# Opening of an encoder kernel: weight row 0, norm gains and token tile 0 as one buffer, loaded by halves of the partitions

## The reference

```
h = concatenate([meta, x], axis=1)            # 272 tokens x 1024
a = rmsnorm(h, g[0])                          # y = x * rsqrt(mean(x*x) + eps) * g
proj = a @ w_in                               # q, k, v, g of 4 heads
q = rotary(q, pos); k = rotary(k, pos)        # cos and sin of position x frequency
```

## Time and profile before

| | |
|---|---|
| median of 3 runs | 696.47 us (696.41 to 696.52) |
| profiled execution, its own time | 696.7 us |
| its span, first to last instruction | 694.9 us |
| TensorE busy | 688.1 us (99%) |
| VectorE busy | 618.9 us (89%) |
| ScalarE busy | 522.3 us (75%) |
| HBM read | 129.23 MB |

### The profile page before, as it was taken

One profiled execution on the slowest core, in us unless ns is written; L12 is line 12 of the kernel. 1 busy time (PEld: TensorE's weight loads), 2 busy tenths in 40 slices (PEclk: granted clock), 3 DMA queues, 4 the chain that ended last, 5 costly groups with the idle time before them and its releaser, 6 DMA issues.

```text
span 694.9 us, 15951 instructions
## 1 busy us (share of the span) xinstructions
PE 688.1 (99%) x6471; PEld 579.0 (83%) x6471; DVE 618.9 (89%) x868; ACT 522.3 (75%) x851; POOL 25.2 (4%) x26
## 2 busy tenths in 40 slices
PE   9999999999999999999999999999999999999997
PEld 7888888888999888888889998888888888884454
DVE  6989898978989799998998889999999999999533
ACT  7477867767755888987888677999878888897441
POOL 0002010100110000000003000000000000000000
PEclk9999999999999999999999999999999999999999
DMA  9875656462643455655589941110545656566821
GB/s 345 325 256 155 246 147 252 139 216 105 220 206 121 154 213 191 232 203 199 202 331 384 354 148 62 62 61 1 182 166 199 237 195 224 199 232 220 256 41 61
DMA packets 48635, 134.51 MB, mean 194 GB/s; under 512 B 30784, under 2 KB 31296, under 8 KB 33344
## 3 DMA queue, kind: packets, MB, share of 16 engines
q1 hardware_dynamic: 48288, 133.39, 54.8%
q10 hardware_dynamic: 288, 0.31, 0.1%
HBM read 129.23 MB, written 1.05 MB: 187 GB/s over the span
## 4 chain that ended last, share of the span: by engine, by line
PE 96%; DVE 2%; DMA 1%; issue 1%; ACT 0%; POOLq 0%; DVEq 0%; SPq 0%; ACTq 0%
PE ps L1894 25%; PE ps L1895 25%; PE ps L1896 25%; PE ps L2397 3%; PE ps L2395 3%; PE ps L2396 3%; PE ps L2329 1%; PE ps L1926 1%; PE ps L1947 1%; PE ps L1927 1%; PE ps L2042 1%; PE ps L2049 1%; PE ps L2044 1%; DMA stage<-in_chunks 1%; PE ps L2145 1%
## 5 line engine op out<-in xcount | busy, mean ns | idle before, releaser
L1894 PE MATMUL ps<-a_hi,w_hi 128*128 128x272 f16 (+1 forms) x1008 | 279.2, 277 | 0.2 <-DVE w_lo L1097 0.2
L1895 PE MATMUL ps<-a_lo,w_hi 128*128 128x272 f16 (+1 forms) x1008 | 279.1, 277 | 0.0
L1896 PE MATMUL ps<-a_hi,w_lo 128*128 128x272 f16 (+1 forms) x1008 | 279.1, 277 | 0.0
L1097 DVE SCALAR_TENSOR_TENSOR w_lo<-stage,w_hi 128x1024 f16<-128x1024 f32 x205 | 247.4, 1234 | 20.6 <-ACT w_hi L566 20.2
L566 ACT ACTIVATE w_hi<-stage 128x1024 f16<-128x1024 f32 x205 | 207.8, 1046 | 49.8 <-PE ps L2397 18.3
L1894 PEld LDWEIGHTS ps<-a_hi,w_hi 128*128 128x128 f16 x1008 | 98.6, 98 | 16.8 <-DVE w_lo L1097 0.5
L1896 PEld LDWEIGHTS ps<-a_hi,w_lo 128*128 128x128 f16 x1008 | 98.6, 98 | 16.1
L1895 PEld LDWEIGHTS ps<-a_lo,w_hi 128*128 128x128 f16 x1008 | 98.6, 98 | 16.0
L1894 PE MATMUL ps<-y_hi,w_hi 128*128 128x272 f16 (+3 forms) x496 | 106.1, 242 | 0.0
L1895 PE MATMUL ps<-y_lo,w_hi 128*128 128x272 f16 (+3 forms) x496 | 106.0, 242 | 0.0
L1896 PE MATMUL ps<-y_hi,w_lo 128*128 128x272 f16 (+3 forms) x496 | 106.0, 242 | 0.0
(11 more groups left out here) (320 smaller groups left out, 1074.9 us busy)
## 6 DMA issues: line engine op xcount, KB each, us to landing
stage<-in_chunks SPq DMA_DIRECT2D x118, 1024.0 KB
work<-work SPq DMA_DIRECT2D x96, 32.0 KB, 2.1
stage<-in_chunks SPq DMA_DIRECT2D x6, 256.0 KB
decay_all<-in_decay SPq DMA_DIRECT2D x1, 1056.0 KB, 11.9
out<-sq SPq DMA_DIRECT2D x4, 256.0 KB, 2.0
hT<-in_tokens SPq DMA_DIRECT2D x3, 272.0 KB, 5.5
stage<-in_chunks SPq DMA_DIRECT2D x1, 512.0 KB
mT<-in_gains SPq DMA_DIRECT2D x1, 512.0 KB, 6.7
```

The costliest lines, as they stand in the source:

```text
L1097: dve.scalar_tensor_tensor(out=part(1, c, q), in0=flat(stage, c, q), scalar=W_SCALE, in1=part(0, c, q), op0=ALU.mult, op1=ALU.subtract).th ...
L1894: pe.matmul(o, w_h, x_h, start=start, stop=False)
L1895: pe.matmul(o, w_h, x_l, start=False, stop=False)
L1896: return pe.matmul(o, w_l, x_h, start=False, stop=stop)
```

## The change

Weight row 0, the norm gains and token tile 0 now stand side by side in one buffer, 512 + 64 + 272 = 848 float32 on each partition, and side by side in the input array too. The upper 64 partitions are loaded by ScalarE's queue, the lower 64 by SP's. ScalarE (for `w_hi` of row 0) and VectorE (for `a_hi` of tile 0) wait until both halves have landed (`x_landed[0]` at 32). SP no longer loads row 0 from the weight array. The place of weight row 0 in the buffer is shared with the rotation table, which is loaded into it later; SP waits for `w_lo` of row 0 (`even_low`) before it issues that load. The total size of the buffers is the same.

```
+OPENING = CW + 8 * DT + T
...
-        hT_all = sb("hT", [P, 8 * DT + DT * T])
-        hT = hT_all[:, 8 * DT:].rearrange("p (a b) -> p a b", b=T)
+        rope_first = sb("rope_first", [P, 2 * T - CW + OPENING + (DT - 1) * T])
+        rope_sb = rope_first[:, 0:2 * T].rearrange("p (a b) -> p a b", b=T)
+        hT_all = rope_first[:, 2 * T - CW:]
+        first_row = hT_all[:, 0:CW]
+        hT = hT_all[:, CW + 8 * DT:].rearrange("p (a b) -> p a b", b=T)
...
-        rope_sb = sb("rope_sb", [P, 2, T])
...
-        gains_sb = hT_all[:, 0:8 * DT]
+        gains_sb = hT_all[:, CW:CW + 8 * DT]
...
-        row_landed = {k: sem(f"row_landed{k}") for k in (0, 1, 2, 4, 5)}
+        row_landed = {k: sem(f"row_landed{k}") for k in (1, 2, 4, 5)}
...
-                at = P * (8 * DT + dt * T)
+                at = P * (OPENING + (dt - 1) * T)
...
             first_chunk = chunks[0:2 * P, :].rearrange("r n -> (r n)")
-            for k0, count in FIRST_ROWS:
+            sp.dma_start(hT_all[0:P // 2, 0:OPENING],
+                         tokens[0:P // 2 * OPENING].rearrange("(p n) -> p n", p=P // 2)).then_inc(x_landed[0], 16)
+            for k0, count in FIRST_ROWS[1:]:
...
                 if c == 1:
-                    sp.dma_start(rope_sb[:], rope).then_inc(table_landed, 16)
+                    sp.wait_ge(even_low, 1)
+                    sp.dma_start(rope_sb, rope).then_inc(table_landed, 16)
                     sp.dma_start(ident_sb[:], ident).then_inc(ident_landed, 16)
...
                     if dt < KC - 2:
-                        if dt in row_landed:
+                        if dt == 0:
+                            act.wait_ge(x_landed[0], 32)
+                        elif dt in row_landed:
                             act.wait_ge(row_landed[dt], 32)
                         else:
                             act.wait_ge(w_landed[0][dt // 4], 32)
-                        act.activation(w_hi[0][:, dt, :], stage[0][:, dt, :], ACTF.Copy,
+                        act.activation(w_hi[0][:, dt, :], stage[0][:, dt, :] if dt else first_row, ACTF.Copy,
                                        scale=W_SCALE).then_inc(whi_made if dt % 2 else even_high, 1)
...
-            for n, (a, b) in enumerate(((0, 8 * DT + T), (8 * DT + T, 8 * DT + 2 * T))):
-                act.dma_start(hT_all[:, a:b], tokens[P * a:P * b].rearrange("(p n) -> p n", p=P)).then_inc(x_landed[n], 16)
+            act.dma_start(hT_all[P // 2:P, 0:OPENING],
+                          tokens[P // 2 * OPENING:P * OPENING].rearrange("(p n) -> p n", p=P // 2)).then_inc(x_landed[0], 16)
+            act.dma_start(hT[:, 1, :], tokens[P * OPENING:P * (OPENING + T)].rearrange("(p n) -> p n",
+                                                                                       p=P)).then_inc(x_landed[1], 16)
...
-            dve.wait_ge(x_landed[0], 16)
+            dve.wait_ge(x_landed[0], 32)
...
-                    dve.scalar_tensor_tensor(out=w_lo[0][:, dt, :], in0=stage[0][:, dt, :], scalar=W_SCALE,
+                    dve.scalar_tensor_tensor(out=w_lo[0][:, dt, :], in0=stage[0][:, dt, :] if dt else first_row, scalar=W_SCALE,
...
-    pieces[0] = np.concatenate([columns(inputs["norm_gains"]), pieces[0]], 1)
+    pieces[0] = np.concatenate([inputs["ret_w_in"][0][0:P, 2 * D:2 * D + CW], columns(inputs["norm_gains"]), pieces[0]], 1)
```

## The result

| kernel | median us | lowest to highest | runs |
|---|---|---|---|
| before | 696.49 | 696.11 to 696.92 | 22 |
| changed | 697.28 | 697.00 to 699.93 | 22 |

What follows compares the result with a forecast made beforehand. TensorE, busy 99% of the span, bounds the kernel; row 0's data hold back its start, at most 0.44 us. Of that 0.33 us was taken to survive row 2, other edits 0: 696.47 - 0.33 = 696.14 us, range 695.8 to 696.9.

Steps and rivals of the forecast that it cites:

- The bound: Start of TensorE's products: at most 0.09 + 0.35 = 0.44 us to win, held back only by row 0's data.
- In the lull the engines lack packets: Opening loads, 2.4 to 2.8 us: half-idle engines at 204 GB/s; 3392 B packets at 120 a us would give 407 GB/s.
- Sharing the opening evenly alone is worth up to 0.36: Opening loads: SP's queue ran ahead of ACT's; an even split would start VectorE near 4.05 us rather than 4.39.
- The opening is through after 434 / 399 = 1.09 us: Opening loads: 434 KB at the full pace of 399 GB/s from about 1.8 us, so VectorE starts at 3.5.
- row 2 decides what passes: Weight row 2: no slack, so only its earlier landing survives as gain; 0.33 us taken, between 0.23 and 0.44.
- The accounting by packets for row 1: Token tile 1: queues share by packets, so 835 KB pass 0.33 us earlier and row 1's w_hi is ready at 5.96.
- Smaller edits at nothing: SP's issue and new wait, buffer placement, w_hi and w_lo work: bounded by -0.1 to +0.1 us, taken as 0.
- That half a transfer's issue might be shorter: SP's queue: if issue goes by partitions, 64 partitions save half an issue, 0 to 0.25 us of SP's time.
- Rival (b): Opening loads: the two halves hinder each other, row 2 starts 0.3 to 0.5 us later, 696.8 to 697.0; chance 0.16.
- they alternate on each engine: Argument against slower halves: both queues would have to be hampered alike throughout, while alternating on each engine.
- The 0.12 us for a product on the lower level: TensorE's first products: one moved onto the 1.2 GHz level would cost 0.12 us; no loss seen, warm-ups stand ahead.
- the case "within": Whole kernel: measured time within 0.2%, 1.4 us, of no change; chance 0.97.

Runs made afterwards that it cites:

- One transfer: Changed kernel, but the whole 848-column opening buffer loaded by one 128-partition transfer on SP's queue: 696.85 us, ratio 1.0005.
- the buffer alone: Changed kernel's shared buffer, layout and SP wait, but the loads of before and ScalarE waiting for the weight row alone: 696.46 us, ratio 0.9999.
- By columns: Changed kernel, but the two queues share the opening buffer as 128 partitions x 424 columns each: 696.70 us, ratio 1.0002.

## Why the prediction was wrong, step by step

- **The bound** (0.44 us to be won at most) was not tested, since no encoder run had its inputs sooner by more than 0.14 us; that row 0 is held by its data stands. It has a reverse side that I didn't use: where nothing is slack, whatever comes late is paid in full.
- **"In the lull the engines lack packets", the opening is through sooner with larger ones: wrong, and here the forecast gain failed.** I read 120 packets a us as a limit in packets. One transfer with the same 3392 B packets moved 148 GB/s from 2.4 to 2.8 us, the changed kernel 178, and the buffer alone 317 with the packets of before. Few packets at half-idle engines were not a sign that wider packets would help, and the lull wasn't even a constant of these loads.
- **"Sharing the opening evenly alone is worth up to 0.36": wrong.** By columns the share is even, and VectorE started at 4.40 against 4.39.
- **The halves taken as equal to whole rows: wrong, and this is what turned no gain into a loss.** "The opening is through after 434 / 399 = 1.09 us" was mis-sized: I took the 399 GB/s of 3.0 to 3.8 us, which are of transfers over 128 partitions, for transfers over 64. Measured by what more bytes cost, one half takes 149 to 157 GB/s and two at once 213, since their queues mostly take turns.
- **Row 1, row 2, and what survives.** That row 2 decides what passes was not borne out: in the changed kernel its w_hi is there 0.23 us before TensorE wants it (8.34 against 8.57), and row 0 alone sets the loss (in one of the profiles with 24 warm-ups TensorE did wait 0.1 us for row 2): 0.65 us at row 1, at row 2 and at 495 us, 0.72 in the medians. The accounting by packets for row 1 had nothing to work on, since row 0 came so late that tile 1 was waiting for ScalarE (its a_hi starts at 5.66 without a wait).
- **Smaller edits at nothing: right within the noise.** The kernel with the shared buffer alone is at 0.9999, and SP reaches the rotation table at 7.45, after w_lo of row 0 (6.08 + 0.68). That half a transfer's issue might be shorter: wrong, it is longer, 0.60 us against 0.39 for 128 partitions in the opening.
- **Rival (b), "the two halves hinder each other", is what happened**, and had 0.16. Its argument against, "they alternate on each engine", is refuted by the queue counts of 2 to 3 us (60 to 2). Its term was mis-sized: ScalarE at 4.7 and row 2 later by 0.3 to 0.5, 696.8 to 697.0, measured 4.97, 0.65 and 697.28. It priced the data's pace by a window of whole transfers; the two halves measured by themselves give the term, 0.85 us. I had the rule of the Trainium skill against the change beside a trace that was silent on it, and gave it too little.
- **The 0.12 us for a product on the lower level** was named and priced right (227 against 116 ns), but as something that wouldn't happen. By the likeliest reading of the table above later inputs make it happen in some runs, up to 699.93 us, and no case of mine held that. The ratio itself, 1.0017, lies inside the 0.2% that the case "within" meant.

## What to carry to other kernels

Split a transfer that is wanted early by columns, not into partitions 0 to 63 and 64 to 127: each half alone takes as long as the whole, and of two at once the second lands 0.8 us behind the first at 217 KB each, 1.8 at 434 KB each. Where a trace shows only whole-width transfers, don't carry their pace over to halves; measure the shape alone: one small kernel gave 0.85 us for what delayed VectorE by 0.66 to 1.09 us in the profiles of the encoder. And look at a window of 0.4 us in a second profile before you build on it. When an input gets later by some tenths of a us, ask as well what TensorE does meanwhile: whether its first products run at the lower level can be worth more than the delay.

## What the runs showed of the hardware beyond that

- 64 rows spread over both sides (32 to 95) beat 64 rows on one by nothing at 54 KB, 0.28 us at 217 KB, 0.9 to 1.0 us at 434 KB.
- A transfer of 64 partitions took 0.47 to 0.54 us to issue, one of 128 took 0.33 to 0.39, and two of 32 together 0.81 to 0.86: fewer partitions do not issue faster. Two halves in a row on SP took 1.23 us.
- The warm-ups' own speed varies between executions: 18 took 4.21 to 4.24 us in six profiles and 3.65 to 3.72 in two, 24 took 5.60 and 4.77. Of the same kernel, then, some executions have part of the warm-ups at the higher level and some none.
